# The scaling of the first softmax block as GpSimd's first operation of a slot, and VectorE's combination of both blocks behind the row maxima of the next step

## What is computed

```
scores  = q_c . k_c                     # two score blocks c = 0, 1 for each head and 128 queries
probs   = softmax(scores)               # over 512 keys
weights = probs[0] - lam * probs[1]
o       = weights @ v
```

## Time and profile before

| | us |
|---|---|
| median of 3 runs | 1360.7 (1360.37 to 1361.06) |
| the profiled execution | 1361.43 |
| its span in the trace | 1359.6 |

### The profile page before, as it was taken

How to read it: one execution, slowest core, us unless ns; L and a number is a source line. 1 busy time by engine, 2 the same in 40 slices (tenths; PEclk the granted TensorE clock), 3 DMA queues, 4 the chain that set the end, 5 groups by cost and what they waited for, 6 DMA issues and landing times.

```text
span 1359.6 us, 20826 instructions
## 1 busy us (share of the span) xinstructions
PE 1339.1 (98%) x7970; PEld 1084.7 (80%) x7970; DVE 911.3 (67%) x1058; ACT 641.9 (47%) x948; POOL 659.5 (49%) x475
## 2 busy tenths in 40 slices
PE   9999999999999999999999999999999999999999
PEld 6778777777888888888877787778788888888887
DVE  7787897665888888600358968975658888885001
ACT  7354667574444444321443546666644444443121
POOL 2553575247444444444565536752564444444443
PEclk9999999999999999999999999999999999999999
DMA  5322222122323333332323222121233323322333
GB/s 188 94 85 80 63 63 71 47 78 85 101 93 99 103 94 93 99 106 93 93 93 93 80 74 68 55 73 45 79 103 98 93 94 103 99 93 93 99 102 109
DMA packets 37140, 121.43 MB, mean 89 GB/s; under 512 B 5056, under 2 KB 5440, under 8 KB 37056
## 3 DMA queue, kind: packets, MB, share of 16 engines
q1 hardware_dynamic: 36768, 119.75, 28.5%
q10 hardware_dynamic: 288, 0.52, 0.1%
HBM read 113.96 MB, written 2.10 MB: 85 GB/s over the span
## 4 chain that ended last, share of the span: by engine, by line
PE 80%; DVE 9%; ACT 4%; issue 4%; POOL 2%; DMA 0%; ACTq 0%; DVEq 0%; POOLq 0%
PE bank L584 24%; PE bank L586 24%; PE bank L585 24%; PE bank L731 2%; DVE QQ L1467 2%; POOL wL L520 1%; PE bank L674 1%; PE bank L749 1%; DVE hL L422 1%; ACT wH L916 1%; PE bank L703 1%; PE bank L740 1%; POOL rstd L434 1%; DVE sqR L1387 1%; PE bank L619 1%
## 5 line engine op out<-in xcount | busy, mean ns | idle before, releaser
L520 POOL TENSOR_TENSOR wL<-raw,wH 128x1024 fp32r<-128x1024 f32 x142 | 343.2, 2417 | 404.3 <-ACT wH L916 294.1
L584 PE MATMUL bank<-hH,wH 128*128 128x512 f32 x1216 | 484.0, 398 | 2.0 <-DVE hL L422 1.8
L586 PE MATMUL bank<-hL,wH 128*128 128x512 f32 x1216 | 474.7, 390 | 0.0
L585 PE MATMUL bank<-hH,wL 128*128 128x512 f32 x1216 | 474.1, 390 | 0.0
L584 PEld LDWEIGHTS bank<-hH,wH 128*128 128x128 f32 x1216 | 228.6, 188 | 66.1 <-issue 14.5
L514 POOL TENSOR_TENSOR wL<-raw,wH 128x256 fp32r<-128x256 f32 x204 | 184.2, 933 | 190.2 <-ACT wH L916 190.2
L586 PEld LDWEIGHTS bank<-hL,wH 128*128 128x128 f32 x1216 | 228.5, 188 | 48.9
L585 PEld LDWEIGHTS bank<-hH,wL 128*128 128x128 f32 x1216 | 228.9, 188 | 45.4 <-issue 0.5
L916 ACT ACTIVATE wH<-raw 128x1024 fp32r<-128x1024 f32 x173 | 182.6, 1056 | 146.4 <-PE bank L586 146.3
L1626 DVE TENSOR_TENSOR x<-x,bank 128x512 f32<-128x512 f32 x16 | 10.9, 682 | 200.7 <-PE bank L586 200.7
L584 PE MATMUL bank<-gH,wH 128*128 (+1 forms) x352 | 137.2, 390 | 0.0
(11 more groups left out here) (172 smaller groups left out, 1730.2 us busy)
## 6 DMA issues: line engine op xcount, KB each, us to landing
raw<-wts SPq DMA_DIRECT2D x210, 512.0 KB, 3.5
x<-xT SPq DMA_DIRECT2D x8, 256.0 KB, 5.7
swp<-K SPq DMA_DIRECT2D x32, 64.0 KB, 2.0
swp<-QO SPq DMA_DIRECT2D x32, 64.0 KB, 2.4
outT<-x SPq DMA_DIRECT2D x8, 256.0 KB, 2.0
raw<-wts ACTq DMA_DIRECT2D x2, 256.0 KB, 4.8
raw<-wts SPq DMA_DIRECT2D x2, 256.0 KB, 5.9
W<-pos SPq DMA_DIRECT2D x1, 256.0 KB, 5.9
```

The costliest lines, as they stand in the source:

```text
L520: pool.tensor_tensor(wL[:, s, :], raw[:, s, :], wH[:, s, :].bitcast(F32), ALU.subtract)\
L584: pe.matmul(out, wH[:, s, a:a + P], rhs_h, start=first, stop=False)
L585: pe.matmul(out, wL[:, s, a:a + P], rhs_h, start=False, stop=False)
L586: return pe.matmul(out, wH[:, s, a:a + P], rhs_l, start=False, stop=last)
```

## The change

The factor of the first block is computed where it was, but its multiplication moves to POOL, and DVE's last two instructions of a step move behind the row maxima of the next step:

- DVE: `combine(a)` is cut in two. `inverses(a)` waits for the exponentials and computes both inverses; it stands where `combine` stood, and signals `inv_sum`.
- POOL: `scale(a)` waits for `inv_sum` and multiplies the first block in place; it is the first job of POOL's slot, ahead of `grow` and of the split. It signals `e_scaled`.
- DVE: the rest of `combine(a)` (the factor with lambda, a wait for `e_scaled`, then W) runs after `row_max` of the next step and before `square_low`. In slot 33, where no next step exists, it stays right behind `inverses`.

```diff
--- before.py
+++ after.py
@@ -296,6 +296,8 @@
         sc_mm = signal("sc_mm", STEPS)
         neg_max = signal("neg_max", STEPS)
         exps = signal("exps", STEPS)
+        inv_sum = signal("inv_sum", STEPS)
+        e_scaled = signal("e_scaled", STEPS)
         w_ready = signal("w_ready", STEPS)
         pv_mm = signal("pv_mm", STEPS)
         od_ready = signal("od_ready", HEADS)
@@ -547,10 +549,17 @@
                             last = pool.tensor_tensor(v, v, w.to_broadcast([P, n, h]), ALU.mult)
                         last.then_inc(hg_k.sem, 1)
 
+                    def scale(a):
+
+                        pool.wait_ge(*inv_sum.at(l, a + 1))
+                        pool.tensor_scalar(E[:, 0, :], E[:, 0, :], sm[:, a, 4:5], None, ALU.mult).then_inc(e_scaled.sem, 1)
+
                     if l == 0:
                         pool.wait_ge(*w_split.at(l, 3))
                     for s in range(SLOTS):
                         n = item_of(s)
+                        if step_of(s - 1) is not None:
+                            scale(step_of(s - 1))
                         if n is not None and 1 <= n % PAIR_ITEMS < LEVELS:
                             grow(*divmod(n, PAIR_ITEMS))
                         if s in SPLITS:
@@ -1505,12 +1514,16 @@
                             m = dve.tensor_reduce(sm[:, a, c:c + 1], bank[4 + c][:], axis=AX.X, op=ALU.max, negate=True)
                         m.then_inc(neg_max.sem, 1)
 
+                    def inverses(a):
+
+                        dve.wait_ge(*exps.at(l, a + 1))
+                        dve.reciprocal(sm[:, a, 4:6], sm[:, a, 2:4]).then_inc(inv_sum.sem, 1)
+
                     def combine(a):
 
-                        dve.wait_ge(*exps.at(l, a + 1))
-                        ch(dve.reciprocal(sm[:, a, 4:6], sm[:, a, 2:4]))
+                        dve.wait_ge(*inv_sum.at(l, a + 1))
                         ch(dve.tensor_tensor(sm[:, a, 6:7], sm[:, a, 5:6], lamc[:, 7:8], ALU.mult))
-                        ch(dve.tensor_scalar(E[:, 0, :], E[:, 0, :], sm[:, a, 4:5], None, ALU.mult))
+                        dve.wait_ge(*e_scaled.at(l, a + 1))
                         if a:
                             dve.wait_ge(*bank6_full.at(l, BANK6[("turn", a - 1)] + 1))
                         dve.scalar_tensor_tensor(W[:], E[:, 1, :], sm[:, a, 6:7], E[:, 0, :], ALU.mult, ALU.add)\
@@ -1530,7 +1543,9 @@
                         if n is not None and n % PAIR_ITEMS == OUT:
                             states(n // PAIR_ITEMS, 1)
                         if step_of(s - 1) is not None:
-                            combine(step_of(s - 1))
+                            inverses(step_of(s - 1))
+                            if step_of(s) is None:
+                                combine(step_of(s - 1))
                         if s == N_IN + 1:
                             low_out(FINISH[N_IN][1])
                         if n is not None:
```

## The result

| | us, median | range | beside it: before |
|---|---|---|---|
| changed kernel, 4 runs | 1381.11 | 1380.94 to 1381.41 | 1360.86 |

The ratio is 1.0148 (95% interval 1.0136 to 1.0160): 20.2 us slower. The forecast said slower, by 8.6 us; the time lies outside its range. The profiled execution took 1381.04 us, its span is 1379.2 (before 1359.6).

A forecast was written before the change was run, and what follows sets the result against it. PE (98% busy) bounds the kernel, DVE costing it only single waits. Terms 2.4 + 2.2 + 2.2 - 0.4 + 1.2 + 1.0 = 8.6 us gave 1369.3 against 1360.7 us, range 1360 to 1375.

The forecast's parts named there:

- the moved pair: Factor and W, now behind the row maxima on DVE: costs 2.4, 2.2 and 2.2 us at slots 20, 22 and 26.
- the price of POOL's queue: Work behind POOL's new wait for the inverses: 1.2 us through slot 23 and 1.0 through slot 33, both layers together.
- the removal from DVE: Multiplication gone from DVE: late slots 0.9 to 1.5 us earlier; only slot 21's wait for W goes away, -0.4 us.
- slot 20, the pair ahead of the query tile: DVE's gapless work behind slot 20's row maxima delays the query tile, PE's 1.83 us wait becomes 3.0: 2.4 us.
- slots 21 to 24 (22: +2.2, 21: -0.4, 23: +1.2): Late eviction behind slot 22's maxima +2.2 us, slot 21's W wait gone -0.4, slot 23's late KK, `kx` and exponentials +1.2.
- behind slot 32 (slot 33): Slot 33 has no row maxima, so DVE waits for POOL: 0.6 us later, taken at 0.5 per layer, 1.0 us.
- I take 1.0, near the KK row.: Duration of POOL's multiplication: 1.0 us, between bounds of 0.5 (half a KK growth) and 1.74 (line 434's two-input sum).
- In slots 21 and 24 the same delay of `kx` ends inside waits of ACT for PE and holds nobody.: ACT's `kx` late behind POOL's KK in slots 21 and 24: ends inside ACT's waits for PE, no cost.
- W itself comes later ...; I take nothing for it.: W ends 0.1 to 0.5 us before PE wants it in slots 19, 22 to 26, 29: nothing taken.
- The rival on POOL's queue: Multiplication takes 1.7 us, KK and exponentials come 0.7 later, transposes wait 0.3 in seven slots: 1376 us, chance 0.14.
- I take 1.2, as POOL is in its KK or its split.: Delay from factor plus W behind the maxima in slots on time: 1.2 us, between 1.0 alone and 1.3 beside POOL.
- ... the scaling costs DVE nothing while it lies beside the maxima.: POOL's multiplication beside DVE's row maxima, which read PSUM: no contention by the skill's rule, so no cost to DVE.

The follow-up runs named there:

- half_scale: The changed kernel with POOL multiplying only the first 256 of the 512 columns, the rest left unscaled: 1375.50 us, ratio 1.0102 to the kernel before.
- w_late_bare: The changed kernel without POOL's multiplication and its two waits, division by the first sum left out: 1367.56 us against 1361.14 for the kernel before.
- no_scale: The kernel before without the 128x512 multiplication on any engine, division by the first sum left out, factor in one instruction: 1357.87 us against 1360.81.
- w_late: The kernel before with only the factor and W moved behind the next row maxima, multiplication still on DVE: 1372.97 us against 1361.18.
- pool_extra: The kernel before, plus POOL waiting for the inverses and multiplying a spare tile in two 256-column pieces at its slot's head: 1375.81 us, ratio 1.0108.
- kx_last: The changed kernel with ACT's `kx` behind the copy of transposed weights and the exponentials in slots with a growth: 1378.88 us, ratio 1.0131.
- pool_wait: The kernel before, plus POOL waiting for the inverses at the head of its slot with no operation behind the wait: 1361.10 us, ratio 0.9999.
- factor_early: The changed kernel with the factor computed right behind the inverses and only W behind the row maxima: 1377.57 us against 1360.81 for the kernel before.
- diagonal: The kernel before without the block multiplication; PE's transposes of W become products by a diagonal of the inverses computed on DVE: 1368.59 us, ratio 1.0056.

## Why the prediction was wrong

The direction, the bound (PE, with DVE costing it only single waits) and the places of the moved pair were right. The size was not, and the step that failed is the price of POOL's queue: 1.2 us for slot 23 and 1.0 for slot 33, 2.2 in all, where the runs show 13.8. Of that, 5.9 is the size of the operation, taken at 1.0 us and measured at 1.57. The rest, some 5.7, is there with an operation of 0.93 us too. By the traces it is what the forecast put at nothing: KK and the splits, pushed back, come to lie on DVE's two-input instructions, and W and the evicted tiles are late for PE (half_scale against w_late_bare: 2.0 and 3.4 us of waits in the first layer against 0.5 and 2.6).

By the parts of the sum, from the corners, each against the kernel before beside it:

| part | forecast | measured |
|---|---|---|
| the removal from DVE | -0.4 | -2.9 (no_scale) |
| the place of the factor and W | 2.4 + 2.2 + 2.2 = 6.8 | +9.4 (w_late_bare less no_scale) |
| POOL's multiplication and its wait | 1.2 + 1.0 = 2.2 | 7.9 + 5.9 = 13.8 (half_scale less w_late_bare, the changed kernel less half_scale) |
| sum | 8.6 | 20.2 (before rounding) |

The first two errors cancel (-2.5 and +2.6), which is luck. Each measured part is uncertain by 1.2 us (the first) to 3.4, and the parts aren't independent: with the multiplication kept on DVE the place of W cost 11.8 (w_late).

The same by slots, with what the slots' starts say:

| step of the forecast | forecast | measured |
|---|---|---|
| slot 20, the pair ahead of the query tile | 2.4 | 1.4 + 1.4 = 2.7 |
| slots 21 to 24 (22: +2.2, 21: -0.4, 23: +1.2) | 3.0 | 4.8 + 4.0 = 8.8 |
| slots 25 to 31 (26: +2.2) | 2.2 | 2.5 + 2.5 = 5.1 |
| behind slot 32 (slot 33) | 1.0 | 1.6 + 1.8 = 3.3 |
| sum | 8.6 | 19.9, less 0.3 gained ahead of slot 17: 19.6 of span |

(Summed before rounding.)

- **"I take 1.0, near the KK row."** The operation took 1.57 us, near the *other* end of the bounds, line 434's sum. The 1.08 us of a KK growth over 512 elements with two inputs had seemed to allow 0.5 for one, and one input was not cheaper than two. Cost: 5.9 us. The estimate taken from the Trainium skill ("GPSIMD Engine Reference", section 3.1), whose 769 ns are the best case of a tight loop over 512 elements, is half of what this instruction took; the measurement decides.
- **"In slots 21 and 24 the same delay of `kx` ends inside waits of ACT for PE and holds nobody."** Wrong for the operation as it is, though not for one of the forecast's size: half_scale, at 0.93 us, has no such wait in either layer. At 1.57 us PE's statistic waited 2.8 us in the first layer and 1.8 in the second. `kx` came after the time at which PE's transposes had filled bank 6, so the copy queued behind it came late and PE's statistic waited. pool_extra shows the wait without the move, kx_last takes it away by order alone. I had followed ACT's queue forward from `kx` to rstd, and not asked which bank the instruction between them frees.
- **"W itself comes later ...; I take nothing for it."** The slack of 0.1 to 0.5 us was read with W at its old duration. W and the factor stretched, and PE waited for W five times in each layer (2.9 and 2.0 us in all), and still 2.0 us in each with the operation at 0.93. The rival on POOL's queue had this wait, at 0.3 each in seven slots; its price of 1376 is 5 us short too, for it had no statistic wait and no stretching.
- **"I take 1.2, as POOL is in its KK or its split."** The pair took 2.3 us in slot 20 (from 151.35 to the end of W at 153.66) and 2.7 in slot 22, though behind slot 20 PE's delay came out near the forecast (1.4 for 1.2): the later two-input work gave time back, T's growth in line 1485 taking 1.29 us where it took 2.25. The relief of 0.4 was 2.9 in all where nothing replaced the multiplication (no_scale); in the changed kernel DVE's busy time shows none left.
- **"... the scaling costs DVE nothing while it lies beside the maxima."** True as far as it goes, and of little use: the maxima stay at 669 to 693 ns, and the scaling costs W and the factor nothing either (pool_extra: W 750 to 755 ns beside it). But only 15.2 of its 50 us lay beside the maxima (in slot 22 it ended at 173.90, and they began at 173.41), and its cost comes by what stands behind it in POOL's queue. That KK and the splits are pushed onto DVE's two-input instructions (23.8 us more of busy time) was in no term. The rule named there (the Trainium skill, "SBUF — State Buffer", Who interferes with whom) has an instruction with two SBUF inputs contend with a GpSimd instruction that reads SBUF. The traces agree for GpSimd's splits and KK, with W up to 1734 ns, and not for its multiplication by a scalar, which reads SBUF too; the measurement decides.
- **Slot 33** came to 3.3 us for 1.0. The chain was the one named: DVE waits 1.56 us for POOL there, in place of an operation of 0.49.

```profile
288.12 1.16 DVE L1529 SCALAR_TENSOR_TENSOR W<-E,sm 128x512 f32<-128x512 f32 x1 [1.56 <-POOL E L555]
```

W too took 1.16 us and not 0.75, beside POOL's split. In the first layer W ends 1.7 us later behind the scores of slot 32 than before; the wait and the longer W are 1.5 of that.

What stays open: of GpSimd's 13.8 us, how much goes over the late KK and how much over DVE's stretched instructions. The statistic's waits are the first kind and taking them away brought 2.5 us net (kx_last); pool_wait shows that KK late by 1.9 us in slot 23 costs next to nothing *alone*, while DVE is less disturbed. The two act on the same late evictions, and no run parts them.

The version that beats both kernels is no_scale, at 1357.87 us (0.25% under the kernel before, with 0.16 to 0.34% as its interval). It takes the multiplication away and gives it to no engine; the division by the first sum scales a whole row of the head's output, and the norm that follows takes such a factor out again, but for its epsilon.

## What to carry to other kernels

Before work is moved to an engine that is idle half the time, write down everything behind its new place in that queue, and follow each to the buffer it frees, across engines, and not only to the next result. Price the operation on the new engine at the dear end if the trace hasn't that very form, and look at which two-input instructions of that engine it pushes onto two-input instructions of VectorE. And compare with the crude version: waiting at the old place was 3.4 us cheaper here than the reordering that was to hide the wait.

## What the runs showed of the hardware

- GpSimd's multiplication by a per-partition scalar took 1567 ns for 128x512 and 927 ns for 128x256 in float32, within 8 ns over 32 executions each. VectorE did the first in 485 at the least, ScalarE in 708.
- A VectorE instruction of one element in each partition, with two inputs, took 142 ns at the least and 1146 at the most, in the changed kernel beside GpSimd's two-input KK. Computing it ahead of the row maxima (factor_early) was worth 3.5 us of the kernel's time.
- GpSimd's multiplication by a per-partition scalar didn't lengthen VectorE's instructions with two SBUF inputs: W of 128x512 took 750 to 755 ns beside it (pool_extra). GpSimd's subtraction of two SBUF tiles (the split) and its product of two (KK) did: 1166 and 1603 ns in the median. VectorE's own multiplication by a scalar, with one SBUF input, took 621 ns in place of 485 beside GpSimd's.
- Four 128x128 float32 products by a diagonal cost PE 0.42 us more than four transposes of the same tiles (diagonal).
- The granted clock of TensorE fell from 2.4 to 1.2 GHz behind a wait of 1.83 us in the second layer of the kernel before, and not behind one of the same length in its first layer. Runs of no_scale with a mean clock of 1.000 and of 0.999 differ by 1.4 us, runs of half_scale with 0.999 to 1.000 and with 0.998 by 1.7.
